# Seven of eight chunks of the down projection as Strassen products, with block sums on GpSimd, and latent value products in two parts

## The reference

```python
u = rmsnorm(h, g_mix);  z = u @ w_in            # latent and differential attention heads
o_mla  = softmax(q @ k.T * scale) @ v            # 8 latent heads, value width 64
o_diff = (softmax(...) - lam * softmax(...)) @ v # 4 differential heads
h = h + concat(o_mla, o_diff) @ w_out
u = rmsnorm(h, g_mlp)
h = h + square(relu(u @ w_up)) @ w_down          # w_up [1024, 4096], w_down [4096, 1024]
```

## Time and profile before

| | |
|---|---|
| median of three executions | 1267.94 us |
| profiled execution, its own time | 1268.16 us |
| its span, first to last instruction | 1266.3 us |
| PE busy | 1238.9 us (98%) |
| VectorE (DVE) busy | 768.0 us (61%) |
| ScalarE (ACT) busy | 507.3 us (40%) |
| GpSimd (POOL) busy | 149.9 us (12%) |
| mean granted TensorE clock | 0.991 of 2.4 GHz |

### The profile page before, as it was taken

The page is one execution under the profiler, slowest core; times in us unless marked ns, Lnnn a source line. Parts: engine busy times, 40 slices in busy tenths (PEclk is TensorE's granted clock), DMA queues, the critical chain, the costliest instruction groups (busy, mean ns, idle before and its releaser), DMA issues.

```text
span 1266.3 us, 15443 instructions
## 1 busy us (share of the span) xinstructions
PE 1238.9 (98%) x5788; PEld 1011.2 (80%) x5788; DVE 768.0 (61%) x1227; ACT 507.3 (40%) x836; POOL 149.9 (12%) x158
## 2 busy tenths in 40 slices
PE   8999899999999999999999998999999999999997
PEld 7887678888888888888878766788888888888886
DVE  5658867666654555455646687775674554455554
ACT  5346657744322222222423466666432222222223
POOL 1001234520000000000000023446000000000000
PEclk8999899999999999999999999999999999999999
DMA  6421101122433333332324220103233333332321
GB/s 184 119 67 59 42 17 34 51 83 74 127 100 96 90 97 100 100 100 93 91 64 107 59 68 8 34 19 98 67 114 98 92 96 100 100 99 88 96 83 66
DMA packets 142779, 103.97 MB, mean 82 GB/s; under 512 B 5442, under 2 KB 138612, under 8 KB 142708
## 3 DMA queue, kind: packets, MB, share of 16 engines
q1 hardware_dynamic: 142480, 102.97, 27.5%
q10 hardware_dynamic: 100, 0.03, 0.0%
q0 software_dynamic: 128, 0.00, 0.0%
HBM read 99.32 MB, written 2.10 MB: 80 GB/s over the span
## 4 chain that ended last, share of the span: by engine, by line
PE 66%; issue 28%; DVE 3%; ACT 2%; DMA 1%; POOL 0%; POOLq 0%; SPq 0%; DVEq 0%; ACTq 0%
PE bank L1207 56%; PE bank L1275 3%; PE bank L1296 2%; PE bank L1247 1%; PE bank L1232 1%; PE bank L1221 1%; DVE pt_lo L891 1%; DMA xin<-in_x 1%; ACT pt_hi L592 0%; PE bank L1376 0%; DMA stage<-in_w_in 0%; PE bank L1368 0%; PE bank L1434 0%; DVE e_x L859 0%; DVE e_t L871 0%
## 5 line engine op out<-in xcount | busy, mean ns | idle before, releaser
L562 ACT ACTIVATE w_hi<-stage 128x1024 fp32r<-128x1024 f32 (+2 forms) x197 | 195.8, 1000 | 490.2 <-PE bank L1207 450.4
L1207 PE MATMUL bank<-u_hi,w_hi 128*128 128x512 f32 x760 | 299.3, 394 | 1.7 <-issue 1.3
L1207 PE MATMUL bank<-u_hi,w_lo 128*128 128x512 f32 x760 | 296.0, 390 | 0.0
L1207 PE MATMUL bank<-u_lo,w_hi 128*128 128x512 f32 x760 | 295.8, 389 | 0.0
L829 DVE TENSOR_TENSOR w_lo<-stage,w_hi 128x1024 fp32r<-128x1024 f32 (+1 forms) x176 | 205.5, 1172 | 58.5 <-ACT w_hi L562 58.4
L1207 PE MATMUL bank<-hid_hi,w_hi 128*128 128x512 f32 x512 | 199.2, 389 | 0.0
L1207 PE MATMUL bank<-hid_lo,w_hi 128*128 128x512 f32 x512 | 199.2, 389 | 0.0
L1207 PE MATMUL bank<-hid_hi,w_lo 128*128 128x512 f32 x512 | 199.2, 389 | 0.0
L1177 DVE TENSOR_TENSOR h<-h,bank 128x512 f32<-128x512 f32 x128 | 87.5, 686 | 136.2 <-PE bank L1207 136.2
L1207 PEld LDWEIGHTS bank<-u_hi,w_hi 128*128 128x128 f32 x760 | 142.7, 188 | 33.7 <-issue 5.1
L1207 PEld LDWEIGHTS bank<-u_hi,w_lo 128*128 128x128 f32 x760 | 142.6, 188 | 30.2
(11 more groups left out here) (186 smaller groups left out, 1562.6 us busy)
## 6 DMA issues: line engine op xcount, KB each, us to landing
stage<-in_w_up SPq DMA_DIRECT2D x64, 512.0 KB, 4.0
stage<-in_w_down SPq DMA_DIRECT2D x64, 512.0 KB, 3.4
stage<-in_w_in SPq DMA_DIRECT2D x32, 512.0 KB, 4.1
stage<-in_w_out SPq DMA_DIRECT2D x16, 512.0 KB, 3.5
xin<-in_x SPq DMA_DIRECT2D x4, 512.0 KB, 7.1
stage<-in_w_ukv SPq DMA_DIRECT2D x4, 512.0 KB, 3.3
out<-yout SPq DMA_DIRECT2D x4, 512.0 KB, 3.6
stage<-in_w_uq SPq DMA_DIRECT2D x4, 384.0 KB, 3.1
```

What stands on the lines that cost most here:

```text
L562: last = nc.scalar.activation(hi(w_hi, s)[:, :, d:d + n], st(r)[:, :, f:f + n], ACT.Copy)
L1207: mm = nc.tensor.matmul(acc, a, b, start=first and t == 0 and m == 0, stop=last and t == len(terms) - 1 and m == 2)
```

## The change

**Down projection, chunks 0 to 6.** The chunk's hidden tile H [512 tokens, 512 channels] is cut into quadrants: A11, A12 are tokens 0 to 255 with channels 0 to 255 and 256 to 511, A21, A22 the same for tokens 256 to 511. The weights [512, 1024] are cut into B11, B12, B21, B22, each [256, 512], held as [128, 1024]. Winograd's form of Strassen's method makes the product with seven block products. The sums, as the code forms them:

The core of the diff:

```diff
-MLP_USES = [f"{kind}{c}_{i}" for kind, c in mlp_order() for i in range(FC if kind == "up" else KD)]
+PRODUCTS = [("A11", "B11"), ("A12", "B21"), ("S2", "T2"), ("S1", "T1"), ("S3", "T3"), ("S4", "B22"), ("A22", "T4")]
+PAIRS = [(2, 3), (0, 1), (5, 7)]
+UP_BANKS, TURN_BANKS = (4, 6), (5, 7, 4, 6)
...
+def low_by(l, b):
+    name, i = BLOCKS[b]
+    return "pool" if name in ("outd", "outm") or is_product(b) and i >= 4 or l > 0 and b < RING else "dve"
...
@@ GpSimd @@
+            def products(l, c):
+                at = BLOCK_AT[(f"down{c}", 0)]
+                pool.wait_ge(hid_f, val(hid_f, l, c * FC + FC))
+                hidden_sum(l, c, "S1", s1[:, :, :], a21(c), a22(c), ALU.add)
+                hidden_sum(l, c, "S3", a21(c), a11(c), a21(c), ALU.subtract)
+                pool.wait_ge(*raw_ready(l, c, "B11"))
+                pool.wait_ge(*raw_ready(l, c, "B12"))
+                if c:
+                    pool.wait_ge(*low_ready(l, BLOCK_AT[(f"down{c - 1}", 3)]))
+                weight_sum(l, c, "T1", t1_w, b12, b11)
+                pool.wait_ge(*raw_ready(l, c, "B22"))
+                weight_sum(l, c, "T3", b12, b22, b12)
+                pool.wait_ge(qa_lo, val(qa_lo, l, 2 * c + 1))
+                hidden_sum(l, c, "S2", a11(c), s1[:, :, :], a11(c), ALU.subtract)
+                hidden_sum(l, c, "S4", a12(c), a12(c), a11(c), ALU.subtract)
+                hidden_low(l, c, "S1", s1[:, :, :])
+                hidden_low(l, c, "S3", a21(c))
+                pool.wait_ge(*low_ready(l, at))
+                weight_sum(l, c, "T2", b11, b22, t1_w)
+                hidden_low(l, c, "S2", a11(c))
+                hidden_low(l, c, "S4", a12(c))
+                pool.wait_ge(*raw_ready(l, c, "B21"))
+                pool.wait_ge(*low_ready(l, at + 1))
+                weight_sum(l, c, "T4", b21, b21, b11)
+                for p in range(4, NP):
+                    out_low(l, at + p)
...
@@ VectorE, before the tiles of up(c) @@
+                    if kind == "up" and c:
+                        dve.wait_ge(qa_hi, val(qa_hi, l, 2 * c - 1))
+                        nc.vector.tensor_tensor(quad_lo[:, 0:2].rearrange("p a k t -> p (a k) t"), raw[:, (c - 1) % 2, :, 0:half],
+                                                quad_hi[:, 0:2].rearrange("p a k t -> p (a k) t").bitcast(F32), ALU.subtract
+                                                ).then_inc(qa_lo, 1)
+                        dve.wait_ge(qa_hi, val(qa_hi, l, 2 * c))
+                        nc.vector.tensor_tensor(quad_lo[:, 2], a22(c - 1), quad_hi[:, 2].bitcast(F32), ALU.subtract
+                                                ).then_inc(qa_lo, 1)
...
@@ PE @@
+                def product(l, c, p):
...
+                    for hf in range(2):
+                        if n >= 3:
+                            pe.wait_ge(prod_read, val(prod_read, l, 2 * (n - 3) + hf + 1))
+                        elif n < 2:
+                            pe.wait_ge(*read_out(l, f"up0_{PAIRS[n][hf]}"))
+                        t = slice(hf * P, (hf + 1) * P)
+                        three(bank[PAIRS[n % 3][hf]][:, :], [((quad_hi[:, q, k, t], quad_lo[:, q, k, t]), wtile(SLOT[b], k, SEQ))
+                                                                 for k in range(2)], True, True).then_inc(prod_done, 1)
...
+                last_down(l, 0)
+                last_down(l, 1)
+                for j in range(0, KD, 2):
+                    last_turn(l, j)
+                    last_turn(l, j + 1)
+                    if j < KD - 2:
+                        last_down(l, j // 2 + 2)
+                for j in range(KD - 3, KD):
+                    last_down(l, j)
...
@@ value products of a latent head @@
-                        mm = nc.tensor.matmul(MISC_BANK[:, :], v_pack[:, kt, hd, :, :].rearrange("p a c -> p (a c)"),
-                                              pt[:, kt, :], start=(kt == 0 and pt is pt_hi), stop=(kt == TT - 1 and pt is pt_lo))
-                mm.then_inc(misc_done, 1)
+                        mm = nc.tensor.matmul(MISC_BANK[:, q], v_pack[:, kt, hd, :, :].rearrange("p a c -> p (a c)"),
+                                              pt[:, kt, q], start=(kt == 0 and pt is pt_hi), stop=(kt == TT - 1 and pt is pt_lo))
+                mm.then_inc(misc_done if half else pv_half, 1)
```

More of the change, by code:

```diff
@@ L123, in mlp_order @@
     return order
-MLP_USES = [f"{kind}{c}_{i}" for kind, c in mlp_order() for i in range(FC if kind == "up" else KD)]
+LAST = CHUNKS - 1
+PRODUCTS = [("A11", "B11"), ("A12", "B21"), ("S2", "T2"), ("S1", "T1"), ("S3", "T3"), ("S4", "B22"), ("A22", "T4")]
+NP = len(PRODUCTS)
+PAIRS = [(2, 3), (0, 1), (5, 7)]
+QUADS = ["A11", "A12", "A22", "S1", "S3", "S2", "S4"]
+SUMS = ["T1", "T3", "T2", "T4"]
+UP_BANKS, TURN_BANKS = (4, 6), (5, 7, 4, 6)
+MLP_USES = [f"{kind}{c}_{i}" for kind, c in mlp_order() if kind == "up" or c == LAST
+            for i in range(FC if kind == "up" else KD)]
 EARLY_USES = LATENT_USES + FIRST_USES + SECOND_USES + FILL_USES
@@ new lines, in last_down @@
+                def last_down(l, j):
+                    use = f"down{LAST}_{j}"
+                    at = BLOCK_AT[(f"down{LAST}", j // 2)]
+                    high, low = block_ready(l, at)
+                    pe.wait_ge(*high)
+                    pe.wait_ge(*low)
+                    pe.wait_ge(*taken(l, use))
+                    pe.wait_ge(prod_read, val(prod_read, l, product_at(LAST - 1, NP - 2 if j < 2 else NP)))
+                    for t in range(FC):
+                        pe.wait_ge(hid_lo_made, val(hid_lo_made, l, t + 1))
+                        w = tuple(x[:, SLOT[at], t * 256 + (j % 2) * P:t * 256 + (j % 2 + 1) * P] for x in (w_hi, w_lo))
+                        mm = three(bank[BANK[use]][:, :], [(w, (hid_hi[:, t, :], hid_lo[t][:, :]))], t == 0, t == FC - 1)
+                    mm.then_inc(proj_done, 1)
@@ new lines, in last_turn @@
+                def last_turn(l, j):
+                    pe.wait_ge(comb_left, val(comb_left, l, 4 if j < TT else 6))
+                    if j >= TT:
+                        pe.wait_ge(comb_right, val(comb_right, l, 4))
+                        pe.wait_ge(turn_read, val(turn_read, l, j - TT + 1))
+                    for tt in range(TT):
+                        mm = nc.tensor.transpose(bank[TURN_BANKS[j % TT]][:, tt * P:(tt + 1) * P], acc[:, tt, j * P:(j + 1) * P],
+                                                 ident[:, :])
+                    mm.then_inc(turn_done, 1)
@@ new lines, in _ @@
+                    elif c < LAST:
+                        for p in range(NP):
+                            product(l, c, p)
+                last_down(l, 0)
[7 more added lines that the diff above has]
+                    last_down(l, j)
+            pe.wait_ge(turn_read, val(turn_read, DEPTH - 1, KD))
```

285 lines of the change are left out of this document (216 added, 69 removed).

## The result

| | before | changed kernel |
|---|---|---|
| median, 20 runs each | 1265.85 us | 1269.88 us |
| lowest to highest | 1262.63 to 1268.59 | 1264.51 to 1274.95 |
| ratio, 95% interval | | 1.0033 [1.0024, 1.0043] |
| profiled execution, its span | 1268.16, 1266.3 | 1274.95, 1273.1 |

The change costs 4.2 us (0.0033 x 1265.9). The profiled execution of the changed kernel is the slowest of its twenty, 5.1 us above their median, and 6.8 us above that of before. Of this, 2.65 us arise ahead of 157 us, where nothing was changed: in the changed kernel's trace PE runs at a granted clock of 0.90 between 32 and 64 us (1.00 before), and at 1.00 between 10 and 20 us (0.74 before). I leave them out.

A forecast was written before the change was run, and what follows sets the result against it. PE, busy 98% of the span, was taken as the bound. Terms -38.1 + 7.0 + 1.8 + 10 + 11.8 + 4.2 = -3.3 us took the profiled 1268.2 and median 1267.9 us to 1265 us, range 1242 to 1279.

The forecast's parts named there:

- (1): Sign, first chunk of a layer: PE gaps of some 2.5 us before up1_2 and 3 us before product 3.
- chunk 0: Term, first chunk of each layer: PE waits while VectorE and GpSimd take turns reading SBUF, +10 us for two layers.
- (4): Sign, down projection: products 0.227 us apart, with no gaps from chunk 1 on.
- rival B: Steady MLP chunks: VectorE's and GpSimd's SBUF reads set a period of 43 to 44 us; 1289 us, chance 0.15.
- (5): Sign, value products: 256-column matmuls come 0.12 us apart.
- value halves: Term, latent value products: 128 matmuls of 512 columns become 256 of 256, costing +1.8 us.
- tail stall: Term, after product 6 of each layer's last Strassen chunk: PE waits 6.8 and 5.0 us for additions, +11.8 us.
- half clock: Term, after each tail stall: PE restarts at 1.2 GHz, some 2.1 us each time, +4.2 us (0 to 7).
- last addition 0.7: Tail step: after product 6, VectorE begins with its last addition, taking 0.7 us, before the last block's split.
- A: Rival, MLP: the SBUF lock is absorbed, chunk 0 costs nothing, tails 2.0 us each; 1243 us, chance 0.28.
- C: Rival, halved value products: bound by the weight load, up to 0.2269 us each; up to 1292 us, chance 0.03.
- D: Rival, MLP: period holds, tail's clock does not matter, chunk 0 is mild; 1257 us, inside the main case (0.50).

The follow-up runs named there:

- e3: Changed kernel, with GpSimd's four corner additions waiting for VectorE's four large additions: 1262.30 us.
- e1: Kernel before, with only the latent value products in two parts of 256 tokens: 1264.75 us, 0.9986 of before.
- e11: Changed kernel, with late corners, the last two down7 splits deferred and squares on ACT, without extra up1 banks: 1248.37 us.
- e5: Changed kernel, with VectorE's low parts of the last two down7 blocks put behind its four large additions: 1262.03 us.
- e9: Changed kernel, with GpSimd's MLP work, except splits of the layers' first blocks, replaced by two constant writes each that read nothing: 1243.53 us.
- e2: Changed kernel, with GpSimd's eight S and T sums a chunk replaced by three constant writes each that read nothing: 1259.72 us.
- e7: Changed kernel, with VectorE scaling and rectifying from PSUM in one instruction and ACT doing the squaring: 1258.56 us.
- e8: Changed kernel, with late corners, the last two down7 splits deferred, squares on ACT and four banks for up1: 1249.55 us.
- e10: As e8, but in chunk 0 GpSimd makes the low part of product 4's block before T4: 1248.05 us.
- e4: Changed kernel, with four PSUM banks instead of two for the four tiles of up1: 1269.17 us, 1.0023 of before.

## Why the prediction was near, and wrong in sign

**The five signs.** (1) The gaps came where they were named. Layer 2 has 3.2 before up1_2, 0.6 before the next tile and 2.7 before product 3, for 2.5, 0.7 and 3.0 in the queue as laid out. Layer 1 has all in one, 4.8: there GpSimd's T1 got in before A22's low part, behind which the first scaling stands, and with PE that late product 3 finds everything ready. That is how this execution went. In e3, with the same code in chunk 0, layer 1 has 2.9, 0.6 and 2.7. (2) The tail gaps were 7.7 and 8.8, for 5 to 8. (3) Splits 2.24 and squarings 1.19 on the mean, PSUM additions 0.68. (4) Steady chunks have no gap. A stretch of the changed kernel:

```profile
core 0: us, PE busy (x) PEld busy (x) DVE busy (x) ACT busy (x) POOL busy (x), PEclk, DMA share, GB/s
...
400.00:560.00 160.00, 160.00 (x708) 132.48 (x706) 127.80 (x126) 60.31 (x68) 129.04 (x60) 1.00 0.34 101
```

PE is busy 160.00 of 160 with GpSimd at 129, so the pair is not the period and rival B is out. (5) 0.12 us.

**The sum**, term by term, over both layers:

| | predicted | measured | from |
|---|---|---|---|
| 168 matmuls | -38.1 | -38.1 | 0.227 apart, no gap in steady chunks |
| transposes | +7.0 | +7.0 | no gap of their own; 0.11 taken over |
| value halves | +1.8 | +0.2 | offset between the traces |
| chunk 0 | +10 | +11.3 | 4.8; 3.2 + 0.6 + 2.7 |
| tail stall | +11.8 | +16.5 | 7.7; 8.8 |
| half clock | +4.2 | +7.6 | 2.5 in chunk 0; 2.3 and 2.8 in the tails |
| wait for a split at the start of layer 2 | 0 | -1.1 | present before, absent after |
| sum | -3.3 | +3.4 | ratio gives +4.2 |

Some 0.8 us are not placed, and the measured column is that of one execution. The half-clock row is the time that transposes and matmuls just behind a gap take over 0.11 and 0.227 us. Windows of the changed kernel, behind the chunk-0 gap of each layer and behind the second tail (columns as above):

```profile
326.00:332.00 6.00, 5.29 (x13) 4.19 (x14) 5.93 (x5) 0.63 (x1) 5.84 (x3) 0.51 0.00 0
...
944.00:950.00 6.00, 5.32 (x24) 4.43 (x24) 5.97 (x4) 1.95 (x3) 5.84 (x3) 1.00 0.00 0
...
1237.00:1243.00 6.00, 5.54 (x17) 4.74 (x18) 5.30 (x9) 2.49 (x4) 0.00 (x0) 0.50 0.00 0
```

The 4.8 us of layer 1 cost the clock (granted 0.51), the 3.2 us of layer 2 did not (1.00). Length alone does not decide it. The MLP stretches of the traces shown here, e1 to e11 included, have 28 gaps of 2.0 to 3.7 us. Over the six us behind each, the mean granted clock was 0.50 to 0.76 in 23 cases and 1.00 in five: in e5 it was 0.72 behind a gap of 2.00 us and 1.00 behind one of 3.43. So part of the half-clock row is chance.

**The step that failed** is the size of the tail, in the words "last addition 0.7": the start of the engines' work there, which measured 3.1 and 4.2 us after the last product. What follows the start was laid out well. From it to the first transpose the queue as laid out has 10.3 us and the traces 10.08 and 10.07, with one corner between any two additions; with this the stall follows: start plus 10.1 less 5.4 gives 7.7 and 8.8 (before rounding). The low part of layer 2's first block, which I added for layer 1, did not step in. So the 7.9 laid out for layer 1 met the measured 7.7 by luck: 2.4 us too much for that low part, 2.4 us too little for the start. Layer 2, without that luck, has 8.8 for 5.6. The late start came through a load: I had VectorE "up to 5 us late" in the steady chunks and the splits' blocks on time, and did not follow what a late split does to the next load of its stage tile. e5 shows that this wait is what cost (3.4 for 7.7 and 8.8), and e9 that it goes when GpSimd doesn't read (2.3 and 2.2).

**A term put at nothing.** The sum has the half clock behind the tails alone. Behind the gap in chunk 0 it came too, for 2.5 us in layer 1, and with the tails the row is 7.6 for 4.2.

**The step that biased the rest** was to shade. I laid out 6.3 us for chunk 0 and 7.9 and 5.6 for the tails, then took 5, 6.8 and 5.0 against the chance that the turns are milder. Unshaded the same sum reads -38.1 + 7.0 + 1.8 + 12.6 + 13.5 + 4.2 = +1.0, on the side where the result fell. In the queues read here the two engines took strict turns whenever both waited. That the forecast is only 5 us off is in part luck: three terms came out cheaper by 1.6 (value halves), 1.3 (chunk 0, unshaded) and 1.1 us (the split), against 3.0 and 3.4 us more for tails and clock.

**The rivals.** A's mechanism is false, and its price is that of the kernel without the reads (e9). B is out by sign 4, C by e1. D is out too: chunk 0 cost 11.3 us and the clock 7.6. The Trainium skill ("SBUF — State Buffer", section on the two separate sides) has VectorE's operations on two SBUF inputs blocked only by GpSimd operations that read SBUF; e2 and e9 agree: VectorE's splits take 1.22 us beside writes, against 2.24 on the mean in the changed kernel.

**Open.** Why the gap of 0.8 us at the start of up1 is absent in e7, e8, e10 and e11; what e1's gain of 1.8 us is; and 0.8 us of the sum. In what order the two engines are let in was read from these queues, not measured by itself.

## What to carry to other kernels

Work given to an idle engine is not free when it holds up a busy one: here GpSimd's reads, with the time that its sums take over plain writes, cost some 26 us, two thirds of the 38 that seven products for eight removed. Give VectorE operations with a PSUM operand, give squares and copies to ACT, and keep GpSimd's reads away while VectorE is on the path that sets the end. In an engine that works in order, look at what stands between the last product and the work that needs it: a split that waits for a late load held finished banks for 1.5 and 2.6 us, and moving it, together with the corners, brought 14.5 us. Ask too what frees the tile that the late load fills: here it was an earlier split, itself held for 1.6 us. If one of several waits has a common cause, more buffers move it and don't mend it (e4).

## What the hardware showed that I had not expected

An operation of VectorE with a single SBUF input is held as well. In e3 the copy of a [128, 512] float32 tile, 0.42 us alone, came while GpSimd ran a low part behind its corners:

```profile
615.44 2.61 DVE L1008 COPY ss<-tmp_s 128x512 f32<-128x512 f32 x1
```

```profile
614.93 2.84 POOL L615 TENSOR_TENSOR w_lo<-stage,w_hi 128x1024 fp32r<-128x1024 f32 x1
```

It ends 0.28 us after GpSimd's operation. In layer 2 the same copy took 1.37 us beside a corner and ended 0.29 us after it. And a waiting engine got in at every hand-over: VectorE's 1.22 us additions and GpSimd's 1.29 us corners alternated at 2.2 us a pair, 0.3 us less than their sum of 2.51, the whole tail long.
